# TensorE's wait for split weights: two pieces at a time in place of one, in a two-layer decoder kernel

## What is computed

```python
for l in range(DEPTH):                      # DEPTH = 2
    h = rms_norm(x, norm_mix_g[l])
    if l % 2 == 0:                          # pooling mixer and HGRN2 recurrence, both gated
        u = h @ w_in_even[e]                # 2048 x 6144
        ...
        x = x + jnp.concatenate([y_a, y_b], axis=-1) @ w_out_even[e]
    else:                                   # stick-breaking attention, gated
        u = h @ w_in_odd[o]                 # 2048 x 8192
        ...
        x = x + (att * jax.nn.silu(gate)) @ w_out_odd[o]
    hx = rms_norm(x, norm_xa_g[l])
    hm = rms_norm(mem, norm_mem_g[l])
    x = x + cross_attention(hx, hm, xa_wq[l], xa_wkv[l], xa_wo[l])
return rms_norm(x, final_norm_g)
```

## Time and profile before

| | |
|---|---|
| median of three runs | 1688.04 us |
| the profiled execution | 1686.34 us |
| its span, first to last instruction | 1684.6 us |
| TensorE matmuls | 9836, busy 1664.0 us |
| VectorE | busy 1115.3 us |
| ScalarE | busy 785.5 us |
| GpSimd | busy 177.8 us |
| memory read | 293.81 MB, 176 GB/s over the span |

### The profile page before, as it was taken

The page is one execution under the profiler, slowest core; times in us unless marked ns, Lnnn a source line. Parts: engine busy times, 40 slices in busy tenths (PEclk is TensorE's granted clock), DMA queues, the critical chain, the costliest instruction groups (busy, mean ns, idle before and its releaser), DMA issues.

```text
span 1684.6 us, 26950 instructions
## 1 busy us (share of the span) xinstructions
PE 1664.0 (99%) x9836; PEld 1456.7 (86%) x9836; DVE 1115.3 (66%) x1188; ACT 785.5 (47%) x924; POOL 177.8 (11%) x122
## 2 busy tenths in 40 slices
PE   7999999999999999999999999999999999999998
PEld 6888888888888888888888888888888888888887
DVE  6765697777776675667765666666666666666554
ACT  5633444455554444435433345554555454444332
POOL 0000041000003410033100000000000013300142
PEclk9999999999999999999999999999999999999999
DMA  8666755555555554457566665556555555644453
GB/s 280 187 188 191 222 172 183 169 172 164 162 174 172 182 172 143 143 163 231 171 197 187 188 188 174 163 161 187 174 168 180 171 166 190 191 153 140 131 185 109
DMA packets 292741, 296.66 MB, mean 176 GB/s; under 512 B 9040, under 2 KB 288848, under 8 KB 292688
## 3 DMA queue, kind: packets, MB, share of 16 engines
q1 hardware_dynamic: 292688, 295.94, 56.4%
HBM read 293.81 MB, written 2.10 MB: 176 GB/s over the span
## 4 chain that ended last, share of the span: by engine, by line
PE 98%; DVE 1%; DMA 0%; ACT 0%; issue 0%; SPq 0%; DVEq 0%; ACTq 0%
PE ps L265 60%; PE ps L267 30%; PE ps L343 2%; PE ps L361 1%; PE ps L287 1%; PE ps L518 0%; PE ps L499 0%; PE ps L508 0%; PE ps L409 0%; DMA xv<-mem 0%; PE ps L432 0%; PE ps L352 0%; PE ps L464 0%; PE ps L459 0%; DVE wpair L813 0%; PE ps L510 0%
## 5 line engine op out<-in xcount | busy, mean ns | idle before, releaser
L813 DVE TENSOR_TENSOR wpair<-raw,wpair 128x1024 fp32r<-128x1024 f32 x544 | 698.2, 1293 | 354.4 <-ACT wpair L569 350.4
L569 ACT ACTIVATE wpair<-raw 128x1024 fp32r<-128x1024 f32 x544 | 574.0, 1059 | 736.0 <-PE ps L267 724.4
L265 PE MATMUL ps<-xpair,wpair 128*128 128x512 f32 x1920 | 679.3, 398 | 0.0
L265 PE MATMUL ps<-ypair,wpair 128*128 128x512 f32 x1536 | 539.9, 397 | 5.6 <-DVE ypair L900 3.0
L267 PE MATMUL ps<-xpair,wpair 128*128 128x256 f32 x1920 | 535.3, 279 | 0.0
L265 PEld LDWEIGHTS ps<-xpair,wpair 128*128 128x128 f32 x1920 | 360.4, 188 | 84.6 <-issue 0.6
L267 PE MATMUL ps<-ypair,wpair 128*128 128x256 f32 x1536 | 428.4, 279 | 0.0
L267 PEld LDWEIGHTS ps<-xpair,wpair 128*128 128x128 f32 x1920 | 361.6, 188 | 0.3
L265 PEld LDWEIGHTS ps<-ypair,wpair 128*128 128x128 f32 x1536 | 288.7, 188 | 74.3 <-issue 6.5
L267 PEld LDWEIGHTS ps<-ypair,wpair 128*128 128x128 f32 x1536 | 289.8, 189 | 0.1
L265 PE MATMUL ps<-wpair,ypair 128*128 128x512 f32 x512 | 179.3, 396 | 0.0
(11 more groups left out here) (182 smaller groups left out, 914.1 us busy)
## 6 DMA issues: line engine op xcount, KB each, us to landing
raw<-xa_wkv SPq DMA_DIRECT2D x128, 512.0 KB, 4.1
raw<-w_in_odd SPq DMA_DIRECT2D x128, 512.0 KB, 4.0
raw<-w_in_even SPq DMA_DIRECT2D x96, 512.0 KB, 3.6
raw<-xa_wq SPq DMA_DIRECT2D x64, 512.0 KB, 3.8
raw<-xa_wo SPq DMA_DIRECT2D x64, 512.0 KB, 3.7
raw<-w_out_even SPq DMA_DIRECT2D x32, 512.0 KB, 3.8
raw<-w_out_odd SPq DMA_DIRECT2D x32, 512.0 KB, 4.2
xv<-mem SPq DMA_DIRECT2D x8, 512.0 KB, 7.2
```

What stands on the lines that cost most here:

```text
L265: mm(bank, still[:, k, 0, tile], move[:, k].rearrange("p h n -> p (h n)"), start=(k == 0), stop=False)
L569: fn(wpair[:, KP * p:KP * (p + 1), 0, :], raw[:, p], ACT.Copy).then_inc(hi_ready, 1)
L813: v.tensor_tensor(wpair[:, kp, 1, :], raw[:, p], wpair[:, kp, 0, :].bitcast(F32), ALU.subtract).then_inc(lo_ready, 1)
```

## The change

TensorE waits for lo_ready at pieces 0 and 2 alone, and there for the split of the piece behind too. Every other wait stays, as do all instructions of the other engines.

```diff
             def piece(c, parity, p, operand, mode, ready=None):
                 if p == 0:
                     pe.wait_ge(evac_done, c + 1)
-                pe.wait_ge(lo_ready, c * 4 + (p + 5))
+                if p % 2 == 0:
+                    pe.wait_ge(lo_ready, c * 4 + (p + 6))
                 if ready is not None:
                     pe.wait_ge(ready[0], ready[1] + 2 * (p + 1))
```

## The result

The changed kernel takes 1700.26 us, the median of five runs between 1697.74 and 1701.79, against 1688.04 for the kernel before (1685.15 to 1691.62). That is 12.2 us more between the medians, beyond the 5.1 us that count as no change, and within the forecast range (1693 to 1702), 2.8 us above the forecast of 1697.5. The ratio on record is 1.0069, 95% interval 1.0048 to 1.009; it follows the means, not the medians, here and in every experiment, so it can differ a little from the quotient of the two medians. Lines of the changed kernel have numbers one higher: L266 is what L265 was in the rows before.

A forecast was written before the change was run, and what follows sets the result against it. TensorE was taken to bound the kernel, busy 99% of the span. Stalls of 8.68 us, less 0.3 for removed waits, plus 1.05 for half rate made 9.5 on 1688.04: 1697.5 us, range 1693 to 1702.

The forecast's parts named there:

- What bounds the kernel: Whole kernel: TensorE is busy 99% of the span, so each microsecond it stands still is paid in full.
- The rival that later pauses swallow a part: TensorE's 4.7 us of later pauses absorb part of the loss, 4.8 us remain: 1692.8 us; chance 0.05.
- Five places, eight late splits: Stalls at chunk 0 pieces 0 and 2, chunk 2, chunk 5 and chunks 18 to 20: 8.68 us in all.
- VectorE's lag of 2 us: Pool stage: VectorE is 2 us behind TensorE, so chunk 18's 1.22 us stall covers chunks 19 and 20.
- the rival of a stall in each pool chunk: Chunks 19 and 20 stall too because VectorE shifts with TensorE, 1.5 us more: 1699.0 us; chance 0.1.
- The removed waits: Pieces 1 and 3: 272 waits for lo_ready go, taken at 0.001 us each, a gain of 0.3 us.
- The rival that the removed waits pay: 272 removed waits at 0.035 us each balance the 9.5 us, time 1688.0 us or less; chance 0.03.
- Piece 0 at half rate: Chunk 0: behind the new pause all of piece 0 runs at half rate, 1.05 us more.
- The clock in the second pause: Pause before piece 2 of chunk 0: clock falls again, 1.4 to 2.8 us more, 1698.9 to 1700.3; chance 0.25.
- the other 264 cost nothing: All 272 pairs of splits: eight come too late for the doubled wait, the others add no time.
- a shift against the kernel before that stays constant: Behind some 260 us the changed kernel's lateness stays at 9 to 10 us to the end.
- a second fall of the clock together with the pool stage: High end of the range: clock falling again before chunk 0's piece 2 plus stalls at chunks 19 and 20, 1701.8 us.

The follow-up runs named there:

- experiment 1: Kernel before, with the doubled wait in chunk 0 alone and single waits elsewhere: 1693.61 us, ratio 1.0031.
- experiment 4: Kernel before with two more, already fulfilled waits in each piece (ScalarE's half and the load), 1088 in all: 1686.05 us, ratio 0.9997.
- experiment 5: Changed kernel with idle 512-column matmuls in the two pauses of chunk 0, 7 before piece 0 and 14 before piece 2: 1698.74 us, ratio 1.0054.
- experiment 3: Kernel before with doubled waits only where there is room, single waits kept in chunks 0 to 7 and 16 to 23: 1692.56 us, ratio 1.0023.
- experiment 9: As experiment 3, but with single waits in chunks 56 and 128 too: 1685.69 us, ratio 0.9994.
- experiment 2: Kernel before with the doubled wait everywhere but in chunk 0: 1696.32 us, ratio 1.0049.
- experiment 10: Kernel before, but in chunks 56 and 128 piece 2 waits for both splits and piece 3 for none: 1688.75 us, ratio 1.0005.
- experiment 11: Changed kernel, but with single waits in chunks 56 and 128: 1697.42 us, ratio 1.0059.

## Why the prediction was right, and where not

- **What bounds the kernel.** Right: what TensorE lost was paid in full, and none of it was taken back by the later pauses for ypair; the shift of experiment 1 stands at 6.65 from chunk 2 to 40 and doesn't shrink at the pauses of chunks 40, 56 and 128. The rival that later pauses swallow a part is out.
- **Five places, eight late splits.** Right in each: forecast 2.94, 2.77, 1.13, 0.62 and 1.22, 8.68 in all; in the first profile 3.05, 2.77, 1.14, 0.72 and 1.18, 8.9. Chunks 19 and 20 did not stall, as VectorE's lag of 2 us had said; the rival of a stall in each pool chunk is out.
- **The removed waits.** 0.3 us were booked as a gain. The 1088 waits that experiment 4 adds cost 1.0 us at most, so 272 are worth 0.3 at the very most, and nothing that was measured. The rival that the removed waits pay is out.
- **Piece 0 at half rate.** Forecast 1.05. The piece itself lost that, and the transposes behind it some tenths where they were cold too: 1.51, 0.92, 0.86 and 0.87 in the four profiles. Right in kind, and experiment 5 shows that it was the clock.
- **The clock in the second pause**, the first rival with a chance of 0.25. It happened in one of four profiles and cost 2.74 us there, inside its price of 1.4 to 2.8.
- **The step that failed**: "the other 264 cost nothing", and with it "a shift against the kernel before that stays constant". They cost no waiting, and the sum had no term for the pace at which pieces run. In both profiles of the changed kernel TensorE stayed at a pace 1.9% slower for the 28 pieces behind piece 3 of chunk 56, where the kernel before was fast both times, and in one of the two for 92 more up to chunk 87. Experiments 3 and 9 differ by the waits of chunks 56 and 128 alone, and the 4.8 us of the first are gone in the second; that the missing wait acts by letting the piece begin 0.09 us earlier is argued, not shown. Against the forecast of 9.5 us the change took 12.2. Stalls and first half rate as forecast, without the 0.3, are 9.7; the slow pieces are worth 5.2 by the means above, too much by 2.7. Experiments 1 and 2 give 5.8 + 8.5 = 14.3. These sums and the 12.2 agree within their intervals (8 to 15 us for the change) and no better.
- **The number and the range.** That 1700.26 lies inside the range is in part luck: its upper end of 1702 was there for a second fall of the clock together with the pool stage, and what filled the room in most profiles was the slow pace, which no rival names.

What stays open: why the two paces exist, and what decides at a given place between them. Shown is where the pace changes, and that putting the single waits back in chunks 56 and 128 took back the loss of experiment 3. The reverse, taking one wait out of each of these two chunks of the kernel before, cost nothing that can be told (experiment 10), and in the changed kernel the mend was not told apart from none (experiment 11). Whether more of the removed waits act on the pace was not tried. No version beat the kernel before by more than can be told: experiment 9 has the lowest median of those run several times, at a ratio of 0.9994 (0.9978 to 1.001).

## What to carry to other kernels

When a wait is widened, hold the end of each producer's instruction against the start of the consumer one step earlier, for all of them: the stalls come out to a tenth of a microsecond, and they are at the start and where the producer is behind, not in the steady state. Removing fulfilled waits gained nothing here. Where a change moves the time though no pause is new, look at the mean duration of the same matmuls in a stretch without pauses: 394 against 399 ns, over 92 pieces, was 4.8 us in this kernel.

## What the runs showed of the hardware

- A stream of alternating 512- and 256-column matmuls, each with its own weights, ran in two steady paces at the same granted clock, 2.773 and 2.825 us for eight pairs. The pace outlasted hundreds of matmuls and changed only behind pauses or other work.
- TensorE's first matmuls ran at half rate (0.64 us a pair against 0.35) until the clock's first entry in the trace, at 14.35 us in the kernel before and at 19.07 to 20.70 us where a pause of some 3 us stood in front of them. With seven idle matmuls in that pause it was at 12.85, and piece 0 ran at full rate.
- In a pause of 3.4 us TensorE's clock fell in one profile, 2.5 us into the pause, and not in three others; it also stayed up in the one profile with 14 idle matmuls there. The Trainium skill, "TensorE: Matmul & The Clock Gate", section "Why this matters for your kernels", warns of such pauses; here one profile agrees and three don't.
- Fulfilled waits, 1088 more of them, cost nothing that can be told: ratio 0.9997 (0.9988 to 1.0006).
